# A three-pass fp32 decoder step on TensorE: low weights before low rows, and a new table of displaced operands

## What is computed

```python
h = x + 0.5 * _swiglu(_rmsnorm(x, norm_ffn1), w1g, w1u, w1d)
u = _rmsnorm(h, norm_mix)
proj = u @ w_in
b_gate, c_gate, v, z_pool, g_conv, g_pool = jnp.split(proj, SPLITS, axis=-1)
conv_y, conv_state = _short_conv(c_gate * v, conv_buf, conv_w)
y_conv = (b_gate * conv_y) @ w_conv_out
pooled, pool_state = _multiscale_pool(z_pool, pool_buf, pos)
y_pool = jnp.einsum('blgc,gcd->blgd', pooled, w_pool_group).reshape(b, L, D_MODEL) * pool_scale
merged = jax.nn.sigmoid(g_conv) * y_conv + jax.nn.sigmoid(g_pool) * y_pool
h = h + merged @ w_o
h = h + 0.5 * _swiglu(_rmsnorm(h, norm_ffn2), w2g, w2u, w2d)
```

## The kernel before

| stage | triples of projections | columns | triples of spreads | columns |
|---|---|---|---|---|
| FFN1 | 1408 | 336 | 704 | 336 |
| pool | 128 | 336 | 32 | 320 |
| convolution | 512 and 256 | 322 and 320 | 256 | 320 |
| mix | 512 | 320 | 256 | 320 |
| FFN2 | 1408 | 320 | 704 | 320 |

## Time and profile before

### The profile page before, as it was taken

The page is one execution under the profiler, slowest core; times in us unless marked ns, Lnnn a source line. Parts: engine busy times, 40 slices in busy tenths (PEclk is TensorE's granted clock), DMA queues, the critical chain, the costliest instruction groups (busy, mean ns, idle before and its releaser), DMA issues.

```text
span 2772.3 us, 47809 instructions
## 1 busy us (share of the span) xinstructions
PE 2757.8 (99%) x18725; PEld 2754.3 (99%) x18725; DVE 1537.4 (55%) x2166; ACT 1052.8 (38%) x1283; POOL 12.4 (0%) x22
## 2 busy tenths in 40 slices
PE   9999999999999999999999999999999999999998
PEld 8999999999999999999999999999999999999998
DVE  6555455554555585555555555575555555555555
ACT  5333333333333453333333334363333333333334
POOL 0000000000000000000000000000000000000000
PEclk9999999999999999999999999999999999999999
DMA  6444444444444445444444444454444444444443
GB/s 198 152 145 144 139 149 144 144 144 144 144 145 144 143 136 153 152 148 143 158 141 159 152 151 144 151 159 152 152 151 151 151 151 151 151 151 151 151 151 106
DMA packets 347876, 412.27 MB, mean 149 GB/s; under 512 B 13039, under 2 KB 283503, under 8 KB 347446
## 3 DMA queue, kind: packets, MB, share of 16 engines
q1 hardware_dynamic: 347264, 410.24, 46.9%
q0 software_dynamic: 560, 1.32, 0.2%
HBM read 408.42 MB, written 3.32 MB: 149 GB/s over the span
## 4 chain that ended last, share of the span: by engine, by line
PE 98%; ACT 1%; DVE 0%; issue 0%; DMA 0%; SPq 0%; ACTq 0%; DVEq 0%
PE bank L433 33%; PE bank L434 33%; PE bank L435 32%; DMA acc<-in_x_sample 0%; ACT tb L742 0%; PE bank L686 0%; ACT w_hi L702 0%; SPq L338 0%; DVE w_lo L957 0%; DVE tok L1029 0%; DVE xn_lo L1010 0%; ACT h L761 0%; DVE h L1126 0%; PE bank L660 0%; ACT acc L783 0%
## 5 line engine op out<-in xcount | busy, mean ns | idle before, releaser
L957 DVE TENSOR_TENSOR w_lo<-raw,w_hi 128x1024 fp32r<-128x1024 f32 x772 | 944.0, 1226 | 1021.9 <-ACT w_hi L702 1021.1
L702 ACT ACTIVATE w_hi<-raw 128x1024 fp32r<-128x1024 f32 x772 | 815.6, 1059 | 1322.3 <-PE bank L435 1321.3
L433 PE MATMUL bank<-xn_hi,w_hi 128*128 128x320 f32 (+2 forms) x4224 | 1314.3, 311 | 2.7 <-DVE xn_lo L1010 2.7
L435 PE MATMUL bank<-xn_hi,w_lo 128*128 128x320 f32 (+2 forms) x4224 | 1304.4, 309 | 0.0
L434 PE MATMUL bank<-xn_lo,w_hi 128*128 128x320 f32 (+2 forms) x4224 | 1303.4, 309 | 0.0
L433 PEld LDWEIGHTS bank<-xn_hi,w_hi 128*128 128x128 f32 x4224 | 793.0, 188 | 3.2 <-issue 3.1
L435 PEld LDWEIGHTS bank<-xn_hi,w_lo 128*128 128x128 f32 x4224 | 792.2, 188 | 0.0
L434 PEld LDWEIGHTS bank<-xn_lo,w_hi 128*128 128x128 f32 x4224 | 792.2, 188 | 0.0
L435 PE MATMUL bank<-hid_hi,w_lo 128*128 128x320 f32 (+1 forms) x1952 | 606.4, 311 | 0.0
L434 PE MATMUL bank<-hid_lo,w_hi 128*128 128x320 f32 (+1 forms) x1952 | 604.7, 310 | 0.0
L433 PE MATMUL bank<-hid_hi,w_hi 128*128 128x320 f32 (+1 forms) x1952 | 598.9, 307 | 0.4 <-issue 0.4
(11 more groups left out here) (109 smaller groups left out, 493.2 us busy)
## 6 DMA issues: line engine op xcount, KB each, us to landing
raw<-in_w_ffn_gate SPq DMA_DIRECT2D x176, 512.0 KB, 3.5
raw<-in_w_ffn_up SPq DMA_DIRECT2D x176, 512.0 KB, 3.5
raw<-in_w_ffn_down SPq DMA_DIRECT2D x176, 512.0 KB, 3.6
raw<-in_w_in SPq DMA_DIRECT2D x176, 512.0 KB, 3.5
raw<-in_w_conv_out SPq DMA_DIRECT2D x32, 512.0 KB, 3.9
raw<-in_w_o SPq DMA_DIRECT2D x32, 512.0 KB, 3.7
raw<-in_w_pool_group SPq DMA_DIRECT2D x4, 512.0 KB, 4.2
out<-acc SPq DMA_DIRECT2D x8, 256.0 KB, 3.1
```

What stands on the lines that cost most here:

```text
L433: pe.matmul(out, slot_hi(n, col, col + P), hi, start=start, stop=False)
L435: return pe.matmul(out, slot_lo(n, col, col + P), hi, start=False, stop=stop)
L702: act.activation(slot_hi(n), raw[:, n % RAW, :], ACT.Copy).then_inc(hi_done, 1)
L957: dve.tensor_tensor(slot_lo(n), raw[:, n % RAW, :], slot_hi(n).bitcast(F32), ALU.subtract).then_inc(lo_done, 1)
```

## The change

The second and the third pass of every triple change places: high by high, low weights by high rows, high weights by low rows. And the tables of displacements are others. In bytes relative to the high weights (which are displaced by 0 in both kernels), modulo 256, with what the first position adds:

| | high rows | low rows by chunk of a projection | low weights by projection of the turn |
|---|---|---|---|
| FFN1 before | 0 | 32, 128, 128, 128 | 0 |
| FFN1 now | 0 | 128, 32, 64, 0 | 0, 32, 64, 128 |
| pool before | 0 | 0 | 0 |
| pool now | 192 | 192, 0, 224, 208 | 0 |
| convolution before | 56 (64 in the last two) | 56 (64) | 32, 192, 192, 192, 32, 32 |
| convolution now | 248 (0) | 248, 56, 24, 8 (0, 64, 32, 16) | 32, 0, 64, 128, 192, 96 |
| mix before | 64 | 64 | 32 |
| mix now | 0 | 0, 64, 32, 16 | 32, 64, 0, 128 |
| FFN2 before | 64 | 64 | 32 |
| FFN2 now | 64 | 64, 128, 96, 192 | 0, 32, 64, 128 |

In the spreads the high rows are at 0 in both kernels. The low rows of `hid` were at 128 in FFN1 and are at 64, 64, 32, 32 by tile in all stages now, as they were in the other stages. The low weights of the eight chunks of a spread were at 0, and are at 0, 32, 0, 32, 64, 64, 128, 128.

```diff
-XH_SHIFT = ((0, 0, 0, 0), (0, 0, 0, 0), (0, 0, 0, 0))
-XL_SHIFT = ((8, 32, 32, 32), (0, 0, 0, 0), (0, 0, 0, 0))
+XH_SHIFT = ((0, 0, 0, 0), (48, 48, 48, 48), (0, 0, 0, 0))
+XL_SHIFT = ((32, 8, 16, 0), (48, 64, 56, 52), (0, 16, 8, 32))
 HH_SHIFT = 5 * ((0, 0, 0, 0),)
-HL_SHIFT = ((32, 32, 32, 32),) + 4 * ((16, 16, 8, 8),)
+HL_SHIFT = 5 * ((16, 16, 8, 8),)
...
-W_SPREAD = 8 * ((0, 0),)
-W_FFN1 = 16 * ((0, 0),) + W_SPREAD
+W_SPREAD = ((0, 0), (0, 8), (0, 0), (0, 8), (0, 16), (0, 16), (0, 32), (0, 32))
+W_FFN1 = 4 * ((0, 0),) + 4 * ((0, 8),) + 4 * ((0, 16),) + 4 * ((0, 32),) + W_SPREAD
 W_POOL = POOL_CHUNKS * ((0, 0),)
-W_CONV = 4 * ((0, 8),) + 12 * ((0, 48),) + 8 * ((0, 8),) + W_SPREAD
-W_MIX = 16 * ((0, 8),) + W_SPREAD
-W_FFN2 = 16 * ((0, 8),) + W_SPREAD
+W_CONV = 4 * ((0, 8),) + 4 * ((0, 0),) + 4 * ((0, 16),) + 4 * ((0, 32),) + 4 * ((0, 48),) + 4 * ((0, 24),) + W_SPREAD
+W_MIX = 4 * ((0, 8),) + 4 * ((0, 16),) + 4 * ((0, 0),) + 4 * ((0, 32),) + W_SPREAD
+W_FFN2 = 4 * ((0, 0),) + 4 * ((0, 8),) + 4 * ((0, 16),) + 4 * ((0, 32),) + W_SPREAD
...
             def three_passes(out, n, col, hi, lo, start, stop):
                 pe.matmul(out, slot_hi(n, col, col + P), hi, start=start, stop=False)
-                pe.matmul(out, slot_hi(n, col, col + P), lo, start=False, stop=False)
-                return pe.matmul(out, slot_lo(n, col, col + P), hi, start=False, stop=stop)
+                pe.matmul(out, slot_lo(n, col, col + P), hi, start=False, stop=False)
+                return pe.matmul(out, slot_hi(n, col, col + P), lo, start=False, stop=stop)
```

## The result

The changed kernel takes 2810.25 us (median; 2810.08 to 2810.42), before takes 2774.71 us. The ratio is 1.0128 with an interval from 1.0112 to 1.0145: 1.3% slower, 35.5 us. I had forecast 2786 us, 12 us more. The sign was right and the time lies in the range, but only by the range's upper end: the loss is three times what I worked out, and my own forecast was to reach no further than 2800 us.

The account below looks back on a forecast made before the run. The prediction took the interval between matmul starts on PE as the bound. Terms of 2.9 + 3.5 + 5.7 = 12.1 us, the others 0, on 2774.16 us gave 2786 us, range 2745 to 2816 us.

Parts of the forecast that it names:

- Rival (a): Operand addresses and pass order cost nothing in this kernel: no change, 2774 us, chance 0.10.
- With one part displaced the rows above carry over: Triples with only low rows or only low weights displaced keep their earlier times in either pass order.
- the rule of 68 slots: FFN1 triples take 68 steps of 6.67 ns where low rows or low weights are at 128, 69 elsewhere.
- FFN1's projections: 1408 triples, 5/16 of a 6.67 ns step more each: +2.9 us, bounds +7.0 and -11.7 us.
- FFN1's spread: 704 triples, three quarters going from 68 to 69 steps of 6.67 ns: +3.5 us, bounds +4.7 and -4.7 us.
- Pool: 128 wide triples staying at 69 steps of 6.67 ns: 0, bounds 0.9 us either way.
- 322 columns: 512 triples staying at 66 steps of 6.67 ns: 0, bounds 3.4 us either way.
- 320 columns: 3424 triples at 65 steps of 6.67 ns, one quarter going to 66: +5.7 us, bounds 22.8 us either way.
- milder form of rival (c): One 6.67 ns step more in nearly every triple, the upper bound: 2813 us, chance 0.14.
- The grid: Every triple's total on PE is a multiple of 6.67 ns, and displacements move it by whole steps or not at all.
- Rival (b): Displaced low weights save 6.67 ns in near three quarters of 6048 triples: 30 us less, 2744 us, chance 0.20.
- Rival (c): With low rows and low weights displaced, PE meets its weight load twice per triple: 60 us more, 2835 us, chance 0.06.

Follow-up runs that it names:

- rows alone: The changed kernel with the low weights' displacement tables of before, keeping the new rows and new order of passes: 2803.84 us, ratio 1.0102.
- weights alone: The changed kernel with the rows' displacement tables of before, keeping the new low weights and new order of passes: 2803.30 us, ratio 1.0101.
- the rotated order: Before with its own tables, passes as low weights, high-high, low rows, the same circle begun one pass earlier: 2779.75 us, ratio 1.0018.
- the kernel with four entries: Before with FFN1's low rows at 128 throughout and low weights of each projection's first chunk at 32, 64, 96, 192, else 0: 2788.08 us.

## Why the prediction was wrong

**What bounds the kernel: right.** PE's interval is all there is, no wait was added, and the exchange by itself is free (ratio 1.000). Rival (a), that addresses cost nothing here, is out: with equal work, tables alone moved the time by 1.4%. The section "Who interferes with whom" of the Trainium skill's page "SBUF — State Buffer" speaks of engines that share ports or don't, and says nothing on addresses. What the measurement decides against is my step from it to a cost of 0; whether PE's two read ports meet here, or what else inside the chip does it, is not shown.

**The step that failed** in the mechanism is the one by which I carried displacements over: "With one part displaced the rows above carry over", and with it the rule of 68 slots wherever one part stands at 128. It took a triple's total for a function of its own addresses. Low rows at 128 with low weights at 0 ran at 460 ns in the changed kernel, and the experiments show 453, 460 and 467 ns for them, by what went ahead. FFN1's projections lost 9.2 us (652.4 us from start to start against 643.2) where I had +2.9, and 7.0 as the upper bound: no cell kept 68 slots, and from the second turn on the mean was 461.5 ns, more than 69 slots. Before's own trace had shown it, in the first turn. The fourth chunk of the first projection and of the second have the same addresses. This is before, chunk starts around the change of rhythm:

```profile
31.42 0.32 PE L433 MATMUL bank<-xn_hi,w_hi 128*128 128x336 f32 x1
...
35.10 0.32 PE L433 MATMUL bank<-xn_hi,w_hi 128*128 128x336 f32 x1
...
38.77 0.31 PE L433 MATMUL bank<-xn_hi,w_hi 128*128 128x336 f32 x1
...
42.40 0.31 PE L433 MATMUL bank<-xn_hi,w_hi 128*128 128x336 f32 x1
```

The chunk at 31.42, rows at 128, took 3.68 us. Then came the one with rows at 32, also about 3.68 us, and from 38.77 on chunks with rows at 128 took 3.63 us for the rest of FFN1. The turn of the earlier trace rows is a later one, where the rhythm was long settled.

**Term by term.** FFN1's spread: +3.5 forecast, +5.0 measured (324.16 against 319.15); the three quarters at 69 slots came, the two chunks with weights at 128 did not keep 68. Pool: 0, measured 0.5 with its wait for the next stage. 322 columns: 0, measured +2.3 (444.6 ns for 440.0); that two "settings that share little" agreed said nothing on the new ones, which are worse than no displacement at all (440.0). 320 columns, the mis-sized term that makes the most of the miss, 13.5 us of 24: +5.7 forecast, +19.2 measured, 5.6 ns per triple where I had 1.67. The value lay close to my upper bound of 22.8. I had written that this width "seems to forgive more", as three settings agreed. But the rows of before show only settings that before uses, and all three are better than no displacement at all, by a slot. Agreement among them said nothing on settings outside them. The milder form of rival (c), one slot more in nearly every triple at 2813 us, came nearest; I had given it 0.14. It came near for another reason than its own, as the last paragraph here says, and that the time lies in the range is owed to it.

**Slips in the text.** I wrote of seven settings, five at 33 or 37 ns above streaming and two at 40; the rows give nine, seven and two. And I took 2% for what a measurement can tell from no change; the interval of 1.0112 to 1.0145 tells 1.3% from none. Neither moves the sum.

**The grid** of 6.67 ns holds in every setting that I had read, but not everywhere. Low weights at 32 with low rows at 128 take 462.5 ns per triple over three whole chunks (rows alone, weights alone), and the rotated order 443.4 ns over a projection. Both are steady, only not within one triple. I had named a total off the grid as what would break my way of counting, and there it does.

**Rival (b)**, displaced low weights save a slot: they do where nothing else is displaced, 433.3 ns with low weights at 32 against 440 at 0, rows at 64 in both, but that is the setting that before had already; among those tried new, rows at 128 with low weights at 64 settled there too, and so did all rows at 0 with low weights at 128 in the changed kernel's mix, while all rows at 0 with low weights at 32 there took 440. Rival (c)'s mechanism, the reversed circle, is not what costs: both orders with the new tables lose 1.3 and 1.4%.

## What to carry to other kernels

When one engine's interval is the bound and it stands in whole steps above streaming, read it at many places, the first turn included, before you call it a property of the operands: here the same triple had three speeds. Settings found in a tuned kernel are likely the good ones, so price an untried setting by the undisplaced case, not by the best rows that you see. Here that would have given 7.0 + 4.7 + 22.8 = 34.5 us more, 2809 us (an estimate from 460.0 and 440.0 ns; the new tables measured 2810 and 2813 us). And where runs of one program fall on two values, print all of them, for a median shows one.

## What the runs showed of the hardware

- The interval of a triple of fp32r matmuls mostly settles on multiples of 6.67 ns, 65 to 67 at 320 columns and 68 to 70 at 336, with the granted clock at 1.00 in the windows of all five stages. Some settings repeat only over two or three triples, with a steady mean between the multiples: 443.4 ns at 322 columns, 462.5 ns at 336. The floor seen is 3 x columns + 80 cycles at 2.4 GHz (433.3 and 453.3 ns); in none of the settings tried at 320 columns did triples settle below it.
- With low rows and low weights where the high ones are, modulo 256 bytes, the total is 460 ns at 336 columns and 440 ns at 320 and 322.
- One program with every triple of a stage alike had two times, 2772 to 2773 us (4 of 10 runs) and 2786 to 2787 us (6 of 10), at equal clock. The medians lie 13.0 us apart; one slot on each of the 2112 triples would be 14.1 us. The profiles of the slower kind show 460 ns throughout; the faster kind has no profile.
- A chunk of eight triples with other addresses can move what follows from one rhythm to another: low rows at 32, or low weights at 96, led to 453 ns, low weights at 192 to 460 ns, low weights at 32 to 467 ns. Behind a wait of PE in the first turn of the kernel with four entries, 467 ns had become 460.
- What in SBUF or PE makes these rhythms, what picks one of the two when a program has no entry, and whether the rotated order's 446 ns at 322 columns comes from the bank change or from its entry, stays open.
